# A two-layer hybrid encoder: other orders of projection, rotation, attention and the first norm

## The reference, cut to what matters

```python
xn = rms_norm(h, attn_norm_g[l])
q, k, v, u = jnp.split(xn @ w_in[l], splits, axis=-1)      # 512, 128, 128, 512 columns
q = apply_rope(rms_norm(q, q_norm_g[l]), cos, sin) * q_scale   # 8 heads of 64
k = apply_rope(rms_norm(k, k_norm_g[l]), cos, sin)             # 2 heads of 64
attn = sliding_sink_attention(q, k, v, sinks[l])    # 16 meta keys and the last two chunks of 64
pool = multiscale_pool(u, w_pool[l], pool_scale[l]) # trailing means over 2, 4, 8, 16, then a map
h = h + jnp.concatenate([attn, pool], axis=-1) @ w_out[l]
# then a gated MLP with a causal convolution, 2816 wide
```

## Time and profile before

| | |
|---|---|
| profiled execution, and span of its trace | 1100.07 us, 1098.3 us |
| runs | 1100.26, 1105.76, 1106.54 us |
| PE busy | 1064.2 us, 97% of the span |
| DVE, ACT, POOL busy | 522.4, 471.3, 123.3 us (48%, 43%, 11%) |
| chain that ended last | PE 82%, ACT 8%, DVE 7% |

### The profile page before, as it was taken

One profiled execution on the slowest core, in us unless ns is written; L12 is line 12 of the kernel. 1 busy time (PEld: TensorE's weight loads), 2 busy tenths in 40 slices (PEclk: granted clock), 3 DMA queues, 4 the chain that ended last, 5 costly groups with the idle time before them and its releaser, 6 DMA issues.

```text
span 1098.3 us, 18457 instructions
## 1 busy us (share of the span) xinstructions
PE 1064.2 (97%) x7668; PEld 1001.0 (91%) x7668; DVE 522.4 (48%) x690; ACT 471.3 (43%) x662; POOL 123.3 (11%) x121
## 2 busy tenths in 40 slices
PE   6998899999999999999999989999999999999997
PEld 6897799999999999999999978999988999888886
DVE  5667645545445545232336576455455544532221
ACT  5775435444444444122237664364344543421110
POOL 1262000111000111000003510000001100000000
PEclk9989999999999999999999899999999999999999
DMA  6311222322322322323321112223223232233212
GB/s 201 103 49 40 77 77 77 103 89 77 114 76 76 105 86 70 103 78 105 104 78 49 39 40 97 96 77 108 84 76 114 77 111 80 76 106 106 72 61 77
DMA packets 93518, 94.30 MB, mean 86 GB/s; under 512 B 3392, under 2 KB 91800, under 8 KB 93480
## 3 DMA queue, kind: packets, MB, share of 16 engines
q1 hardware_dynamic: 92768, 93.01, 26.4%
q0 software_dynamic: 400, 0.58, 0.2%
q10 hardware_dynamic: 312, 0.18, 0.1%
HBM read 91.65 MB, written 2.10 MB: 85 GB/s over the span
## 4 chain that ended last, share of the span: by engine, by line
PE 82%; ACT 8%; DVE 7%; issue 1%; DMA 1%; SPq 0%; POOL 0%; DVEq 0%; ACTq 0%; POOLq 0%
PE slot L443 80%; ACT probs L919 3%; ACT w_hi L337 1%; DVE nmax L1170 1%; DMA x_in<-in_x 1%; ACT rot_s L844 1%; DVE ms_work L1121 1%; DVE probs L1189 1%; DVE w_lo L348 1%; DVE mix_lo L1205 0%; ACT x_hi L778 0%; DVE den L1181 0%; DVE sumsq L1046 0%; DVE sink_arg L1175 0%; ACT pool_hi L852 0%
## 5 line engine op out<-in xcount | busy, mean ns | idle before, releaser
L443 PE MATMUL slot<-x_hi,w_hi 128*128 128x264 f32 (+1 forms) x1552 | 364.1, 302 | 5.4 <-DVE x_lo L1033 2.7
L443 PE MATMUL slot<-x_lo,w_hi 128*128 128x264 f32 (+1 forms) x1552 | 361.0, 300 | 0.0
L443 PE MATMUL slot<-x_hi,w_lo 128*128 128x264 f32 (+1 forms) x1552 | 360.2, 299 | 0.0
L348 DVE TENSOR_TENSOR w_lo<-raw,w_hi 128x2048 fp32r<-128x2048 f32 (+2 forms) x87 | 194.6, 2237 | 247.6 <-ACT w_hi L337 247.6
L337 ACT ACTIVATE w_hi<-raw 128x2048 fp32r<-128x2048 f32 (+3 forms) x89 | 160.8, 1806 | 260.8 <-PE slot L443 259.5
L443 PEld LDWEIGHTS slot<-x_hi,w_hi 128*128 128x128 f32 x1552 | 254.4, 190 | 17.4 <-DVE u_sb L1152 3.9
L443 PEld LDWEIGHTS slot<-x_lo,w_hi 128*128 128x128 f32 x1552 | 253.0, 190 | 7.3
L443 PEld LDWEIGHTS slot<-x_hi,w_lo 128*128 128x128 f32 x1552 | 252.6, 191 | 7.4
L443 PE MATMUL slot<-m_hi,w_lo 128*128 128x264 f32 (+1 forms) x528 | 140.7, 321 | 0.0
L443 PE MATMUL slot<-m_hi,w_hi 128*128 128x264 f32 (+1 forms) x528 | 140.4, 320 | 0.0
L443 PE MATMUL slot<-m_lo,w_hi 128*128 128x264 f32 (+1 forms) x528 | 140.3, 320 | 0.0
(11 more groups left out here) (142 smaller groups left out, 931.3 us busy)
## 6 DMA issues: line engine op xcount, KB each, us to landing
raw<-in_w_gate SPq DMA_DIRECT2D x44, 512.0 KB, 4.6
raw<-in_w_up SPq DMA_DIRECT2D x44, 512.0 KB, 4.4
raw<-in_w_down SPq DMA_DIRECT2D x32, 512.0 KB, 4.3
raw<-in_w_in SPq DMA_DIRECT2D x19, 512.0 KB, 4.9
raw<-in_w_out SPq DMA_DIRECT2D x16, 512.0 KB, 4.5
raw<-in_w_down SPq DMA_DIRECT2D x16, 384.0 KB, 3.6
x_in<-in_x SPq DMA_DIRECT2D x4, 512.0 KB, 7.7
out<-y_out SPq DMA_DIRECT2D x8, 256.0 KB, 3.0
```

Source lines behind the costliest of these rows:

```text
L348: ins = nc.vector.tensor_tensor(w_lo[s][:, a:b], raw[s][:, a:b], w_hi[s][:, a:b].bitcast(f32), ALU.subtract)
L443: ins = nc.tensor.matmul(out_part, w[ws][:, r, cols], a[:, k, tokens], start=first and n == 0 and w is w_hi and a is a_hi, stop=end and w ...
```

## The change

What it does, part by part:

1. The first norm of layer 0 is taken from the token rows of x: ACT squares each row tile with a running sum (`row_ms`), takes a root, DVE inverts it, and PE spreads it over the partitions. The eight squares of `h` and their sums go for that norm.
2. The order on PE becomes k, q0, q1, q2, q3, u3 and, behind scores(0), v; the transposes of v come behind scores(1). The columns of `w_in` are grouped into other units for it. The five side rows ahead of the attention go behind it: `SIDE_ENDS` gives steps 1 to 7 seven rows or six.
3. The swaps of the rotation are transfers between parts of SBUF on SP's queue, four each, and sine, cosine and swap buffers are doubled.
4. On DVE `row_maxima` comes first in a step, then the meta copy, `divide` and `heads_lo`. On ACT `probs_out` comes before `heads_hi`.
5. PSUM slots are assigned anew, and the pooled groups come as 3, 0, 2, 1 instead of 3, 2, 1, 0.

The diff, cut to its core:

```diff
+        order = [("k", 2), ("attn_norm", 0), ("q0", 3), ("k_sq", 2), ("q1", 1), ("q2", 0), ("qn0", 2), ("q3", 3),
+                 ("u3", 1), ("qn1", 2), ("v", 3), ("v_T", 2)]
...
-            sine = v_T[:]
-            rot_c = sb(sc, "rot_c", [P, L])
-            rot_s = sb(sc, "rot_s", [P, L])
+            sine = [v_T[:], run_b[:, PAD:]]
+            rot_c = [sb(sc, f"rot_c{n}", [P, L])[:] for n in range(2)]
+            rot_s = [sb(sc, "rot_s", [P, L])[:], run_a[:, PAD:]]
...
-        GROUPS = (3, 2, 1, 0)
+        GROUPS = (3, 0, 2, 1)
-        SIDE_ENDS = [5, 8, 14, 20, 26, 32, 38, 44, 48, 48, 48, 48, 48]
+        SIDE_ENDS = [0, 0, 7, 14, 21, 28, 34, 41, 48, 48, 48, 48, 48]
...
+                def shift(n):
+                    sp.wait_ge(sine_ready, l * 5 + (n + 1))
+                    if n >= 2:
+                        sp.wait_ge(*rotated(l, n - 2))
+                    for to, fr in ((0, 32), (32, 0), (64, 96), (96, 64)):
+                        sp.dma_start(rot_s[n % 2][to:to + 32], sine[n % 2][fr:fr + 32])\
+                          .then_inc(rots_ready[n % 2], 16)
...
+                load(l, U_VU0, win[:, :, col_v:col_v + UC])
+                shift(0)
+                shift(1)
+                load(l, U_U12, win[:, :, col_v + UC:col_v + 2 * UC])
+                for n in range(2, 5):
+                    shift(n)
...
                 for step in range(NB + 2):
                     if step < NB:
                         scores(step)
+                    if step == 0:
+                        project("v", U_VU0)
+                    if step == 1:
+                        v_transposed()
...
             for t in range(SEQ // P):
...
+                act.wait_ge(x_loaded[t], 16)
+                nc.scalar.activation(y_out[:, t], x_in[:, t], ACT.Square, accum_out=row_ms[:, t:t + 1])\
+                  .then_inc(row_summed, 1)
...
+                if t == 3:
+                    act.wait_ge(row_summed, 5)
+                    nc.scalar.activation(row_ms[:], row_ms[:], ACT.Sqrt, bias=eps[:], scale=1.0 / D_MODEL)\
+                      .then_inc(row_root, 1)
                 act.wait_ge(filled[t], ps.PROLOGUE[t])
...
                 for step in range(NB + 3):
+                    if step < NB:
+                        row_maxima(step)
+                    if step == 0:
+                        dve.wait_ge(*shifted(l, 4))
+                        scaled("v", v_T[:])
                     if 3 <= step < NB + 2:
                         meta_probs_out(step - 2)
+                    if 1 <= step <= NB:
+                        divide(step - 1)
                     if step >= 3:
                         heads_lo(step - 3)
...
-                    if 1 <= step <= NB:
-                        divide(step - 1)
-                    if step < NB:
-                        row_maxima(step)
```

More of the change, by code:

```diff
@@ L481, in _ @@
             pe.wait_ge(h_copied, SEQ // P)
+            s = ps.slot("attn_norm")
+            pe.wait_ge(evac[s], ps.before("attn_norm", 0))
+            pe.wait_ge(row_inv, 1)
+            for t, (bank, c0, n) in enumerate(ROW_TILES):
+                ins = nc.tensor.matmul(slot[s][:, bank, c0:c0 + n], row_ms[0:n, t:t + 1].broadcast_to([n, P]),
+                                       ident[0:n, 0:n], start=True, stop=True)
+            ins.then_inc(filled[s], 1)
             eight = [(k, k) for k in range(KT)]
@@ L528, in project_side @@
                         (g, half), name = HALF_TILES[i], side_name(i)
-                        unit = U_U01 if g < 2 else U_U23
+                        unit, c = {0: (U_VU0, 1), 1: (U_U12, 0), 2: (U_U12, 1)}[g]
                         if k == 0:
                             open_slot(name, l)
-                            if g == 1 and half == 0:
+                            if g == 2 and half == 0:
                                 pe.wait_ge(lo_split[unit % 2], slot_turn(l, unit) + 2)
-                        ins = dense(None, unit % 2, (g % 2) * P, [(k, k)], x_hi, x_lo, part=half,
+                        ins = dense(None, unit % 2, c * P, [(k, k)], x_hi, x_lo, part=half,
                                     first=k == 0, last=k == KT - 1)
@@ L626, in _ @@
                         pool_map(3)
-                rows = [(k, k) for k in (7, 6, 5, 0, 1, 2, 3, 4)]
+                rows = [(k, k) for k in (7, 4, 6, 0, 1, 2, 3, 5)]
                 def mixed(k):
@@ L799, in _ @@
                 gain_hi(0, R_AG, k)
+            s = ps.slot("attn_norm")
+            act.wait_ge(filled[s], ps.before("attn_norm", 0) + 1)
+            nc.scalar.activation(rinv[:, 0:N_META + 3 * P], slot[s][:, 0, 0:N_META + 3 * P], ACT.Copy)
+            nc.scalar.activation(rinv[:, N_META + 3 * P:], slot[s][:, 1, 0:P], ACT.Copy).then_inc(evac[s], 1)
             act.wait_ge(raw_loaded[0], 32)
-            nc.scalar.activation(w_hi[0][:, :, P:UC], raw[0][:, :, P:UC], ACT.Copy).then_inc(hi_split[0], 1)
+            nc.scalar.activation(w_hi[0][:, :, 0:P], raw[0][:, :, 0:P], ACT.Copy).then_inc(hi_split[0], 1)
             split_hi(act, 0, 1)
-            for k in range(KT):
-                square(0, 0, k)
-            act.wait_ge(eps_ready, 1)
             act.wait_ge(prep_ready, 1)
@@ L1114, in _ @@
                 scaled("k", k_dup[:, 0])
-                scaled("v", v_T[:])
                 q_tile(0)
                 dve.wait_ge(qtab_ready, l + 1)
-                dve.wait_ge(evac[ps.slot("v_T")], ps.before("v_T", l) + 1)
                 sine_part(0)
+                split_lo(dve, l, 2)
                 dve.wait_ge(evac[ps.slot("k_sq")], ps.before("k_sq", l) + 1)
```

245 lines of the change are left out of this document (126 added, 119 removed).

## The result

The changed kernel takes 1123.91 us (median of 4 runs, 1122.21 to 1125.02); the kernel before, run beside it, 1103.01 us (1099.05 to 1106.54). The ratio is 1.0189 with a 95% interval of 1.0144 to 1.0234: slower by about 1.9%, as forecast (1121, range 1099 to 1131). The interval lies clear of 1; whether the loss is over 2% it leaves open. The profiled execution took 1124.38 us, with a span of 1122.6 us against 1098.3 before, and a mean granted clock of 0.981 against 0.988.

What follows compares the result with a forecast made beforehand. PE, busy 97% of the span, was taken as the bound. 1100.1 + 16.1 + 7.2 + 4 - 5.2 - 5.1 + 0 + 1.6 = 1118.7; 2 more for spread gave 1121 us, range 1099 to 1131.

Steps and rivals of the forecast that it cites:

- The ring through slot 3: Attention steps, scores 2 to scores 8: `heads_lo` waits for PE's scores, PE's heads for slot 3; together +16.1 us.
- The tail: Scores 8 to output projection: about 16.95 us against 14.0 and 12.6 before, so +2.9 and +4.3, +7.2 us.
- The clock: Attention tails: low PE clock behind an idle piece of 4.2 us; 2 us per layer between 0 and 3, +4 us.
- The front: Ahead of scores 2: seven side rows per layer moved out, -5.2 us, and less low clock, -5.1 us.
- The waits of the front: Waits for squares, sums and rotation ahead of the attention: taken as 0, ends -4 and +10 us.
- The prologue: Kernel start: ACT's last square, table load and root delay PE's k, with nothing covering it; +1.6 us.
- The waits go: Attention steps: slot 3 released before PE finishes its rows ahead of the heads, waits vanish; 1089.5 us, chance 0.10.
- The steps overlap more: Attention steps and tail: more overlap than counted, half of 27.3 us remains; 1107 us, chance 0.16.
- The clock falls through the attention: Attention: two 10 us stretches per layer at low clock, +9.6 us beyond the 4 counted; 1131 us, chance 0.10.
- The transfers are late: Swaps on SP's queue stand behind loads, first scores wait 5 us more per layer; 1131 us, chance 0.08.

Runs made afterwards that it cites:

- fillers: Changed kernel plus 14 and 26 matmuls that nobody reads, in PE's waits ahead of heads(6) and heads(7): 1116.73 us, ratio 1.0137.
- The version with the old order: Changed kernel with DVE's step back to meta copy, `heads_lo`, division, maxima, all else kept: 1102.69 us, ratio 1.0012.
- the version that starts k at 18.08: Row norms' products moved behind k's projection, against the changed kernel with DVE's previous order and third pooled tile rounded in step 7: 1095.96 us, ratio 0.9958.

## Why the prediction was right, point by point

- **The sum.** By the traces the loss was 24.3 us where the terms gave 18.6; the 2 us added for the spread of the kernel before brought the forecast to 1121. Of the 5.7 us that were short, 1.2 lie in the steps, 2.7 in the tail with its clock and 2.4 in the front, less 0.6 behind the second attention. The range of 1111 to 1130 "from the ends of clock and waits" isn't the plain sum of those ends, and its making isn't given.
- **The ring through slot 3.** Right in mechanism; that the size fits so well is in part luck. The steps of layer 0 took 6.05, 7.43, 8.84, 6.54, 6.18 and 5.81 us where 6.0, 7.8, 7.4, 6.7, 6.3 and 6.0 were forecast; the one that is 1.4 us too long, scores(4) to scores(5), ran partly at half clock (its transposes at 97.85 took 1.06 us against 0.60). Layer 1 has the same in the step before (8.96 us, and then 7.28). With 7.43 and 7.28 for these two steps the six last 39.3 us and not 40.2: the ring alone is worth +14.2 against +16.1, and the clock in the steps, put at nothing, another +3.1. Sum 17.3. Waits for `mix_lo`: 27.0 us, "some 20" forecast.
- **The tail.** Heads(7) were put at 10.1 us after scores(8) and came at 10.65 in layer 0, behind an idle piece of 4.2 us, as forecast, in both layers. The whole tail was put at 16.95 and took 16.8 us once the clock was held up by fillers: +7.0 for the term of +7.2.
- **The clock.** The term that was mis-sized: 4 us were counted for the tails, and the fillers took 6.9 out of them. I took 2 us a layer between 0 and 3; layer 1 lost 4.5, outside these ends: there even the heads at 688.09 and the maps behind them were at half clock. With the steps' 3.1 the clock cost 10 us. The reason given does not hold either: I laid it on the wait of 4.2 us, and the clock fell behind the one of 2.2. The version with the old order, whose longest wait in the tail is 1.7 us, has 0.55 through 120 to 128 as well.
- **The front.** Forecast -10.3 for rows and clock, measured -6.3 with the prologue in it. The rows' 5.2 are the count of rows moved; no run isolates them. The clock in front gave less: 595 to 605 rose to 1.00, but behind scores(0) it stayed low, and 65 to 70 had 0.50 in layer 0. Other versions with the same front have scores(2) of layer 0 as early as 75.56 instead of 78.99. So a gain of the front has to be read over several versions, and which of them is typical is not shown.
- **The waits of the front**, put at 0 in the sum: k's scaling comes 5.8 us sooner (38.12 to 32.34), and scores(0) waits 1.2 us for `q_rot` in each layer, 0.9 once before. Zero was close enough. A swap was put at 4 us against 2.6 on ACT, and takes 4.0 where nothing else holds it up (issued from 58.02, used at 61.99): the page shows 2.0 us from issue to landing (rows below), and the four issues alone hold SP's queue for 2.41 us.
- **The prologue**, +1.6 with "nothing covers it". Here the reasoning failed, in a small term. PE's k did start later, by 2.1 us (19.57), with 2.61 us of row norm products ahead of it. (The expectation above has them at half clock. PEclk reads 1.00 through 17 to 22 in this trace, while k's products there come every 0.22 us, so their clock isn't settled.) But "nothing covers it" was wrong: k's result lies until the constants land at 32.34, DVE idle for 4.43 us, and it is from there that the chain to scores(0) runs. The term is nothing, and the version that starts k at 18.08 gained nothing. The root itself went as the earlier trace rows was read, one load followed by its activation at once (rows below).
- **The rivals.** *The waits go* needed a chain on DVE of under 2.5 us; it is 3.0 (102.12 to 105.15). *The steps overlap more* fell with the same rows. *The clock falls through the attention* was right in part: one step of each layer and both tails, worth 6 us more than the 4 counted, against the 9.6 of that rival. *The transfers are late* fell: no wait at scores(0) over 1.2 us. One wait was not foreseen: 1.7 us of transposes behind ACT's copies of v's windows.

The rows of the swaps in the page of the changed kernel (how many, KB each, us to landing), and ACT's timeline at the root of the row norms:

```profile
rot_s<-v_T SPq DMA_DIRECT2D x24, 66.0 KB, 2.0
run_a<-run_b SPq DMA_DIRECT2D x16, 66.0 KB, 2.0
```

```profile
14.90 1.28 ACT L840 ACT_TABLE_LOAD   x1
16.19 0.30 ACT L840 ACTIVATE row_ms<-row_ms,eps 128x5 f32<-128x5 f32 x1
```

## What to carry to other kernels

On an engine that runs in order, look for the operation that frees a buffer for another engine, and what is put ahead of it. An edit that puts one output (the maxima) ahead of some 1.5 us of other work cost 29 us in the kernel before, because the release then waited for the very engine that waits for the release. Ask of each moved step not only who wants its result but who wants its slot, and close the ring on paper: if every member of it depends on the one before, the step time is the plain sum. And other effects of the same edit can hide under such a loss, so time the parts apart. The rest of this change was level with the kernel before (1.0012), in part because a gain in front met a later rounding in the tail, and with that one rounding put back it was worth 0.7%.

## What the runs showed of the hardware that I had not expected

- Idle pieces of 2 to 4 us on PE cost something behind them too: 40 useless matmuls per layer in those pieces made the kernel 7.2 us faster and its tails 2.3 and 4.5 us shorter. In the version with the old order the tails with 15 in waits of 0.9 and 1.4 us were 1.4 us shorter in the trace, but one tail without any was as short.
- A queue holds up a small transfer by more than its issue. The 66 KB shift issued at 47.87 behind a load of weights was used only at 54.30 (POOL had waited 7.27 us for it), where the last of the layer, with no load just ahead of it, was used 4.0 us after its issue began. With the order of shift and load swapped, this shift was used 4.0 us after its issue began too (47.33 to 51.37).
- The clock behind scores(0) differs between programs whose instructions are the same up to there, and is worth 1.5 to 2.9 us a layer, as much as most of the edits here. One profile can't decide between versions that differ by 3 us.
- The start of layer 0's attention hangs on the landing of one table of constants in nine of twelve versions: scores(0) starts 31.3 to 31.4 us behind the scaling of k that waits for it, wherever between 30.97 and 32.35 us that begins.
